# Two-layer hybrid decoder trunk: the projections that end a sub-layer computed token-major with 512 weight columns moving, and turned back by transposes behind two filler units

## What is computed

```
for layer in range(2):
    g = norm_gains[layer]
    h = rmsnorm(x, g[0])
    m = mixer_ab(h, ...) if layer == 0 else mixer_cd(h, ...)   # ends in  mix @ w_out
    x = x + rmsnorm(m, g[1])
    h = rmsnorm(x, g[2])
    x = x + rmsnorm(cross_attn(h, mem, ...), g[3])             # ends in  o @ wo
    h = rmsnorm(x, g[4])
    x = x + rmsnorm(sq_relu_mlp(h, w1, w2), g[5])              # relu(h @ w1)**2 @ w2
```

## Time and profile before

| | |
|---|---|
| time of three runs | 931.27, 933.71, 935.31 us (median 933.71) |
| profiled execution | span 935.2 us, of which no more is outside than the 0.1 us to the longest run |
| PE busy | 890.5 us (95%) |
| DVE, ACT, POOL busy | 638.7 (68%), 468.9 (50%), 173.9 us (19%) |
| DMA | 154.92 MB, mean 166 GB/s |
| granted TensorE clock | 0.990 of full |

### The profile page before, as it was taken

One profiled execution on the slowest core, in us unless ns is written; L12 is line 12 of the kernel. 1 busy time (PEld: TensorE's weight loads), 2 busy tenths in 40 slices (PEclk: granted clock), 3 DMA queues, 4 the chain that ended last, 5 costly groups with the idle time before them and its releaser, 6 DMA issues.

```text
span 935.2 us, 17320 instructions
## 1 busy us (share of the span) xinstructions
PE 890.5 (95%) x7354; PEld 866.8 (93%) x7354; DVE 638.7 (68%) x1006; ACT 468.9 (50%) x663; POOL 173.9 (19%) x165
## 2 busy tenths in 40 slices
PE   8899998999999999999989998999998799999996
PEld 7899998998989999999889988899998799999996
DVE  4686996687497555554779999855884675555552
ACT  6664554565465444444543333365653554444443
POOL 1120800000001000000048778655000010000000
PEclk9999999999999999999999999999999899999999
DMA  8454434544555656655645665444632355655551
GB/s 297 130 179 135 136 122 149 181 136 142 166 178 177 198 183 192 190 184 178 199 127 178 196 183 181 136 160 156 194 122 90 115 180 186 191 185 181 185 176 46
DMA packets 82821, 154.92 MB, mean 166 GB/s; under 512 B 6822, under 2 KB 8760, under 8 KB 82744
## 3 DMA queue, kind: packets, MB, share of 16 engines
q1 hardware_dynamic: 82632, 153.77, 52.3%
q10 hardware_dynamic: 112, 0.05, 0.0%
HBM read 151.58 MB, written 1.05 MB: 163 GB/s over the span
## 4 chain that ended last, share of the span: by engine, by line
PE 66%; DVE 21%; ACT 6%; POOL 2%; issue 2%; DMA 2%; DVEq 0%; SPq 0%; POOLq 0%; ACTq 0%
PE ps L556 20%; PE ps L557 20%; PE ps L558 20%; DVE w_lo L1420 8%; ACT w_hi L1036 3%; DVE ps L1765 2%; DMA raw<-in_ab_w_in 2%; POOL w_lo L2050 2%; DVE tmp L1703 1%; DVE h_lo L1431 1%; DVE xc L1487 1%; DVE xT L1710 1%; PE ps L778 1%; DVE cv L1938 1%; PE ps L918 1%
## 5 line engine op out<-in xcount | busy, mean ns | idle before, releaser
L1036 ACT ACTIVATE w_hi<-raw 128x1024 fp32r<-128x1024 f32 x284 | 295.2, 1054 | 231.4 <-DMA raw<-in_mlp_w 130.7
L1420 DVE TENSOR_TENSOR w_lo<-raw,w_hi 128x1024 fp32r<-128x1024 f32 x238 | 290.7, 1244 | 141.0 <-ACT w_hi L1036 137.0
L556 PE MATMUL ps<-h_hi,w_hi 128*128 128x256 f32 x1248 | 353.0, 283 | 20.8 <-DVE w_lo L1420 11.3
L557 PE MATMUL ps<-h_lo,w_hi 128*128 128x256 f32 x1248 | 349.9, 280 | 0.0
L558 PE MATMUL ps<-h_hi,w_lo 128*128 128x256 f32 x1248 | 349.8, 280 | 0.0
L556 PEld LDWEIGHTS ps<-h_hi,w_hi 128*128 128x128 f32 x1248 | 238.5, 191 | 25.2 <-DVE w_lo L1420 12.4
L558 PEld LDWEIGHTS ps<-h_hi,w_lo 128*128 128x128 f32 x1248 | 237.1, 190 | 0.0
L557 PEld LDWEIGHTS ps<-h_lo,w_hi 128*128 128x128 f32 x1248 | 236.8, 190 | 0.1
L556 PE MATMUL ps<-r_hi,w_hi 128*128 128x256 f32 x512 | 144.3, 282 | 0.0
L558 PE MATMUL ps<-r_hi,w_lo 128*128 128x256 f32 x512 | 144.1, 281 | 0.0
L557 PE MATMUL ps<-r_lo,w_hi 128*128 128x256 f32 x512 | 144.1, 281 | 0.0
(11 more groups left out here) (269 smaller groups left out, 1252.4 us busy)
## 6 DMA issues: line engine op xcount, KB each, us to landing
raw<-in_mlp_w SPq DMA_DIRECT2D x128, 512.0 KB, 3.8
raw<-in_cd_w_in SPq DMA_DIRECT2D x40, 512.0 KB, 3.9
raw<-in_xa_wkv SPq DMA_DIRECT2D x32, 512.0 KB, 3.8
raw<-in_ab_w_in SPq DMA_DIRECT2D x24, 512.0 KB, 4.5
raw<-in_xa_wq SPq DMA_DIRECT2D x16, 512.0 KB, 4.0
raw<-in_xa_wo SPq DMA_DIRECT2D x16, 512.0 KB, 3.8
raw<-in_cd_w_out SPq DMA_DIRECT2D x16, 512.0 KB, 3.9
raw<-in_ab_w_out SPq DMA_DIRECT2D x12, 512.0 KB, 3.7
```

The costliest lines, as they stand in the source:

```text
L556: nc.tensor.matmul(dst, wt[0], x[0], start=start, stop=False, skip_group_check=True)
L557: nc.tensor.matmul(dst, wt[0], x[1], start=False, stop=False, skip_group_check=True)
L1036: nc.scalar.activation(w_hi[:, v % SLOTS, :, :], raw[:, v % SLOTS, :, :], ACT.Copy)\
L1420: V.tensor_tensor(w_lo[:, v % SLOTS, :, :], raw[:, v % SLOTS, :, :], f(w_hi[:, v % SLOTS, :, :]), ALU.subtract).then_inc(lo_ready_dve, 1)
```

## The change

All 108 units of `out`, `wo` and `w2` go through a new function `tokens`: 128 tokens of the activation are stationary, 512 weight columns move, and the result is token-major. ACT's squares then sum over a row by themselves (`accum_out`), so that `token_sums`, `rows`, `Ssum` and `Nrow` go at boundaries. The factor is made for each half of the tokens, ACT and DVE write the normed result `mt`, PE turns it back by 16 transposes behind the second filler unit, and DVE makes `xT` from PSUM in one operation a block. The last sub-layer's 16 transposes go; its gains come as a broadcast row (`gpost`) by one more DMA on SP. PSUM banks are dealt out anew.

```diff
-SETS = {0: dict(M0=(2, 3), M1=(0, 1), FI=(4, 5), T=(6, 7)),
-        1: dict(M0=(0, 1), M1=(4, 5), FI=(2, 3), T=(6, 7))}
+M0, M1, FI, T_ = (2, 3), (0, 1), (4, 5), (6, 7)
...
+            def tokens(seg, dest, src, k0=0, first_k=True, last_k=True, ready=None, only=None, tail=2):
+                def products(u, i, t, kt, start, stop):
+                    hi, lo = (x[:, t * P:(t + 1) * P] for x in src(kt))
+                    wh, wl = w_hi[:, u % SLOTS, i, :], w_lo[:, u % SLOTS, i, :]
+                    dst = bank(dest[t])
+                    nc.tensor.matmul(dst, hi, wh, start=start, stop=False)
+                    nc.tensor.matmul(dst, hi, wl, start=False, stop=False)
+                    return nc.tensor.matmul(dst, lo, wh, start=False, stop=stop)
...
+                    for t in range(TT):
+                        for q in range(kts):
...
             def boundary(l, n, filler):
-                filler([0])
-                pe.wait_ge(dve_made, after("dve", "S2", l, n))
-                token_sums(("nstat", l, n), halves(S2))
-                filler([1])
-                pe.wait_ge(pool_made, after("pool", "nr", l, n))
-                rows(("nrow", l, n), [rfac[:, 1 + 3 * l + n, t:t + 1] for t in range(TT)])
+                filler([0, 1])
+                for i in range(4):
+                    if i == 0:
+                        pe.wait_ge(act_made, after("act", "mt", l, n, 1))
+                    if i == 2:
+                        pe.wait_ge(dve_made, after("dve", "mt", l, n, 1))
+                    transposes(("mT", l, n, i), [((c * TT + t) * P, mt[:, t, (2 * i + c) * P:(2 * i + c + 1) * P], P)
+                                                 for c in range(2) for t in range(TT)])
                 filler([2, 3])
```

ACT's `boundary`, behind its `round_to(x + 1)`:

```diff
-                    for i in range(4):
-                        act.wait_ge(*full(m[i]))
...
+                    squares(n, m, 0)
+                    squares(n, m, 1)
+                    round_to(x + 2)
+                    squares(n, m, 2)
+                    normed(n, m, 0)
+                    squares(n, m, 3)
                     round_to(x + 3)
+                    normed(n, m, 1)
+                    new_h(tag, gl, gs, nxt)
+                    round_to(nxt + 5)
```

`new_x` on DVE, and the new DMA on SP:

```diff
-                        V.scalar_tensor_tensor(out=tmp[:, j % 2, :], in0=bank2(m[j // 2])[:, j % 2, :],
-                                               scalar=gain(l, 2 * n + 1, j), in1=Nrow[:, :], op0=ALU.mult,
-                                               op1=ALU.mult).then_inc(dve_made, tick("dve", "dx", l, n, j))
+                        V.scalar_tensor_tensor(out=xT[:, j, :], in0=bank2(("mT", l, n, j // 2))[:, j % 2, :],
+                                               scalar=gain(l, 2 * n + 1, j), in1=xT[:, j, :], op0=ALU.mult,
+                                               op1=ALU.add).then_inc(dve_made, tick("dve", "x", tag, j))
...
+                if u == first[("w1", 1, 2)]:
+                    sp_.dma_start(gpost[:, :], A["norm_gains"][1, 5:6, :].broadcast_to([P, D])).then_inc(gpost_landed, 16)
```

More of the change, by code:

```diff
@@ L361, in trunk @@
             otok = sb("otok", [TT, D], scope=s)
-            mg = sb("mg", [J, T], scope=s)
+            mg = sb("mg", [TT, D], scope=s)
+        with ExitStack() as s:
+            skip(42432, s)
+            mt = sb("mt", [TT, D], scope=s)
+            gpost = sb("gpost", [D], scope=s)
         ps = ctx.enter_context(nc.psum_tensor("ps", [P, 8, 512], F32))
@@ L901, in _ @@
                 if l == 0:
[L902 removed]
+                    tokens(("out", 0, "early", 0), out_banks(0, 0), mix0, k0=ke, last_k=False,
                             ready=mix_ready(0))
@@ L932, in _ @@
                     token_sums(("varstat",), halves(S2))
-                    project(("out", 1, "early", 1), out_banks(1, 1), mix1, k0=ke, last_k=False, only=[3])
+                    tokens(("out", 1, "early", 1), out_banks(1, 1), mix1, k0=ke, last_k=False, only=[3])
                     pe.wait_ge(pool_made, after("pool", "lnr"))
@@ L963, in wo @@
                     k0 = 0 if part == "early" else 4
-                    project(("wo", l, part, g), [("wo", l, g, 0), ("wo", l, g, 1)], h_src, k0=k0,
-                            first_k=part == "early", last_k=part == "late", only=only,
-                            ready=lambda kt: pe.wait_ge(dve_made, after("dve", "o", l, kt // 2)))
+                    tokens(("wo", l, part, g), [("wo", l, g, 0), ("wo", l, g, 1)], h_src, k0=k0,
+                           first_k=part == "early", last_k=part == "late", only=only,
+                           ready=lambda kt: pe.wait_ge(dve_made, after("dve", "o", l, kt // 2)))
                 if l == 0:
@@ L2026, in _, with weighted @@
             low_to(NU)
-            norm_sum(1, 2, m)
-            factor(1, 2)
-            dve.wait_ge(pool_made, after("pool", "nr", 1, 2))
-            for i in range(4):
+            def weighted(i):
                 g, t = i // 2, i % 2
-                dve.wait_ge(*full(("mout", g, t)))
-                dve.wait_ge(act_made, after("act", "xout", g, t))
-                V.scalar_tensor_tensor(out=otok[:, t, 512 * g:512 * g + 512], in0=bank(("mout", g, t)),
-                                       scalar=rfac[:, 6, t:t + 1], in1=otok[:, t, 512 * g:512 * g + 512],
-                                       op0=ALU.mult, op1=ALU.add).then_inc(dve_made, tick("dve", "otok", i))
+                V.tensor_tensor(mg[:, t, 512 * g:512 * g + 512], bank(m[i]), gpost[:, 512 * g:512 * g + 512], ALU.mult)\
+                    .then_inc(dve_made, tick("dve", "mg", i))
+                freed("dve", m[i])
+            dve.wait_ge(gpost_landed, 16)
+            for t in range(TT):
+                norm_left(1, 2, t)
+                weighted(t)
+            for t in range(TT):
+                norm_right(1, 2, t)
+                weighted(2 + t)
+                dve.wait_ge(pool_made, after("pool", "nr", 1, 2, t))
+                own()
+                for g in range(2):
+                    dve.wait_ge(act_made, after("act", "xout", g, t))
+                    c = slice(512 * g, 512 * g + 512)
+                    V.scalar_tensor_tensor(out=otok[:, t, c], in0=mg[:, t, c], scalar=rfac[:, 6, t:t + 1],
+                                           in1=otok[:, t, c], op0=ALU.mult, op1=ALU.add)\
+                        .then_inc(dve_made, tick("dve", "otok", 2 * t + g))
         @block.gpsimd
```

293 lines of the change are left out of this document (146 added, 147 removed).

## The result

| | before | after |
|---|---|---|
| median | 933.72 us (931.27 to 935.31, four runs) | 922.53 us (922.05 to 923.04, four runs) |
| ratio | | 0.9887, 95% interval 0.987 to 0.9903 |
| profiled span | 935.2 us | 920.9 us, in an execution of 922.89 us |
| PE, DVE, ACT busy | 890.5, 638.7, 468.9 us | 884.9, 626.2, 472.8 us |

What follows compares the result with a forecast made beforehand. It took PE's stream of matmuls and its waits (66% of the chain) as the bound. Terms -10.2 + 2.7 - 6.5 - 1.5 - 3.7 = -19.2 us put the median at 914.5 us, range 907 to 922.

Steps and rivals of the forecast that it cites:

- Step 1: New 512-column matmuls of `out`, `wo` and `w2` at about 227 ns: -10.2 us, bounds nil and -11.6.
- (d): Something in the `r` tiles holds each new matmul up; slower from 246 ns, 943 us at 250; chance 0.03.
- Rival (b): Pace goes by columns alone, the stationary load being hidden at 256 columns too; Step 1 lost, 924.5 us; chance 0.06.
- Rival (e): 256-column streams keep one of two paces; `w1` of layer 1 shifting means 911.5 or 917.5 us; 0.73 with forecast.
- Step 3: PE's stops behind the boundaries, laid to DVE's `w_lo` order, nearly all recovered: -6.5 us, bounds 0 and -6.8.
- Rival (a): DVE stays late behind the boundaries, with no slack at `nxt+1`; most of Step 3 lost, 920 us; chance 0.12.
- Step 4: Boundary (1,1), no filler: `mt` at E+3.4, PE restarts at E+5.9: -1.5 us, bounds -2.4 and 0.
- Steps 2 and 5: Four boundaries with filler, 16 transposes at each: +2.7 us; the end, last `otok` at E+3.4: -3.7 us.
- Rival (c): Sixteen transposes let the clock fall, 2 us at each of five boundaries: 924.5 us; chance 0.06.

Runs made afterwards that it cites:

- r192: Changed kernel with `r_hi` and `r_lo` 128 bytes further up in SBUF, at byte 0 of 256; 920.1 us, ratio 0.9865.
- r256: Changed kernel with `r_hi` and `r_lo` 192 bytes further up in SBUF, at byte 64 of 256; 922.42 us in one run.
- kick: r192 with one identity transpose ahead of each `w1` group from the third on; 917.71 us, ratio 0.9825.
- combo_kick: Changed kernel with the edits of r192 and low4, reordered squares and `w_lo` at (1,1), and identity transposes ahead of 13 `w1` groups; 910.74 us, ratio 0.9741.
- combo_warm: combo_kick with 22 identity transposes at (1,1) ahead of PE's wait for `mt`; 910.69 us, ratio 0.9747.
- wlo4: Changed kernel with three `w_lo` ahead of the new x and ACT's w_hi moved forward, at the four boundaries with filler; 923.06 us, ratio 0.9879.
- low4: Changed kernel with `w_lo` of the fifth unit, `nxt+4`, ahead of DVE's waits at (0,2); 920.7 us, ratio 0.9868.

## Why the prediction was wrong

The direction was right, and the size too large by 8 us. Against the second trace of before it is by 10, since about 2 us of the gain lie ahead of the first changed matmul; that they fell on the forecast's side is luck. By its own steps, between the first trace of before and that of after:

| step | forecast | measured |
|---|---|---|
| 1, pace of the new matmuls | -10.2 | -5.4: `w2` -4.1, `out` layer 1 -1.5, layer 0 -0.2, `wo` +0.4 |
| 1, what was left out: `w1` of layer 0 | 0 | +2.5 |
| 2, work at four boundaries | +2.7 | +3.0 |
| 3, stops behind them | -6.5 | -2.2 |
| not in it: attention of layer 1 | 0 | -2.1 |
| 4, boundary (1,1), with the clock behind it | -1.5 | -0.7, and -1.9 |
| 5, the end | -3.7 | -4.5 |
| sum (of unrounded terms) | -19.2 | -11.4 |

Against the second trace of before, `w1` of layer 1 is a further line, with 0 forecast and +2.9 measured, and the sum is -8.9; smaller differences of the two traces make the other 0.4.

**Step 1 failed in its size.** It took V's 226.7 ns, measured with `mem` stationary, for `w2`, where `r` is. `w2` ran at 232 and r192 and r256 show that the position of `r` in SBUF sets that. The row was right and did not hold for another address. The tiles that I could place fit it at 512 columns: 227 to 228 at byte 0 of 256 (`mem`, `mh`, and `r` in r192), 229 at 192 (`h`), 232 at 128 (`r`), 233 at 64 (`my`, `mp`, and `r` in r256). Only `r` was moved by experiment. The working had noticed that `w2` ran 5 ns slower than `wo`, but used it only for a rival near 246 ns, (d). That one was right that something about `r` holds the new matmuls up, and wrong in the size. Rival (b), twice the old pace whatever is stationary, came out for two of the projections: `out` of layer 0 at 233 for 2 x 117.7 and `wo` at 229 for 2 x 113.8. The Trainium skill's formula for the gap of a single matmul (215.8 ns, "TensorE: Matmul & The Clock Gate", "Back-to-back issue gap") stays below every pace seen, and the 3.3 us that the working took from it is 3.2 by its own numbers.

**Rival (e) came true with its sign against the change.** The six `w1` groups behind a `w2` in layer 0 went from 10.89 to 11.31 us. Layer 1's ran at 11.31 already in the first profile, but at 10.89 in the second of before, so a typical execution loses there too, up to 2.9. What puts a stream into one pace or the other is not settled; a single 128-column transpose brought it back to 113.5 in 9 of 12 groups of kick, 11 of 13 of combo_kick and 12 of 13 of combo_warm, and a stop of 0.2 us did in the changed kernel at (0,0).

**Step 3 was right that the stops behind the boundaries go, had their cause in part wrong, and missed one wait.** The stops went, as forecast. But wlo4, with three `w_lo` ahead of the new x again, has none either, so the order of `w_lo` that the term is built on did not decide it. The working for DVE's list covered four units, `nxt` to `nxt+3`, "for 18.3 and 21.2", and ended there. Behind (0,2) DVE next waits twice for other engines, and the new list had left the fifth unit behind these waits. It cost 3.2 us of idle time, and then a half clock, and low4 gives 3.6 of it back. Rival (a) named another cause. In layer 1 the shorter list freed DVE early enough that the transposes of the probabilities wait 1.55 us less, a gain that I had not looked for.

**Step 4 had the wait right and the clock wrong.** `mt` came at E+3.4. The forecast then put the first bank at E+4.1 and the restart at E+5.9 with transposes at full speed. They ran at half clock and cost 1.6 more. "I leave this as it is" was also wrong: the transposes took the slow time on themselves, and the matmuls behind them got 1.9 back.

**Steps 2 and 5** held: 16 transposes took 1.66 us with no wait ahead, and the last `otok` ended at E+3.2 for E+3.4; a landing 0.6 us shorter than the 3.0 assumed, for which I have no cause, makes most of the rest. Rival (c) fell, since the clock stays at 1.00 through the transposes at the four boundaries with filler; the half clock behind (0,2) begins in PE's wait of 3.2 us. Its working was also wrong that no stretch of before has so many transposes in a row. There is one, and the window 40.3 to 42.4 around it reads a clock of 1.00:

```profile
40.67 1.94 PE L623 MATMUL ps<-ident,memtok 128*128 128x128 f32 x16
```

## What to carry to other kernels

A matmul's pace read at one tile isn't good for another: read it for the operand that will be stationary, or give that operand the same place in a 256-byte line as the one that was measured. Where a list that feeds PE is rewritten, count not only the units whose need comes first but also the last one that must be through before the engine's next wait on others; that is where 3.6 us went. A wait of PE of some 3 us cost more than its length here, as the clock fell with it (3.2 us at (0,2) and at (1,1)), and a stop of 0.2 us at (0,0) cost nothing, as it reset a slow pace. So judge a wait by what the stretch gains without it, not by its own length. And take two profiles of the kernel before: here one and the same program differed by 3.4 us, nearly a third of the gain.

## What the runs showed of the hardware

The matmul's pace depends on where the tile lies: 226.7, 231.9 and 233.3 ns at 512 columns for `r` at bytes 0, 128 and 64 of 256. Streams of 256 columns, same tiles and same code, hold 113.5 or 117.8 ns for a whole group of 96, may differ between two executions of one program, and could be reset by one small instruction in 32 of 38 tries. A row of 38 transposes over 4.3 us held the granted clock at 1.00, where it fell to half behind 2.3 us without work. A POOL operation on one column takes 0.54 us alone and 1.46 beside a DVE operation that reads two tiles.
